# Modulation rows as column-tiled matmuls of four halves at once, made in the attentions and beside the context mixer

## The reference, cut to what matters

```
for l in range(2):                                       # first block
    mod = silu(c) @ w_ada[l] + b_ada[l]                  # 1024 x 6144
    sh_m, sc_m, gt_m, sh_f, sc_f, gt_f = split(mod, 6)
    h = rms_norm(x, g_pre_mix[l]) * (1 + sc_m) + sh_m
    x = x + gt_m * rms_norm(token_mixer(h), g_post_mix[l])
    h = rms_norm(x, g_pre_ffn[l]) * (1 + sc_f) + sh_f
    x = x + gt_f * rms_norm(conv_glu_ffn(h), g_post_ffn[l])
for i in range(2):                                       # second block
    mod_l = split(silu(c) @ w_mod[i] + b_mod[i], 6)      # the tokens' rows
    mod_c = split(silu(c_ctx) @ w_mod[i] + b_mod[i], 6)  # the context's rows
    ...
```

## Time and profile before

| | us |
|---|---|
| median of three runs | 3613.68 (3610.74 to 3615.86) |
| the profiled execution | 3609.14 |
| its span, first to last instruction | 3607.8 |
| TensorE busy | 2909.2 (81%) |
| VectorE busy | 2291.7 (64%) |
| ScalarE busy | 1138.5 (32%) |
| mean granted clock of TensorE | 0.912 |
| DMA | 1108.81 MB, mean 307 GB/s |

### The profile page before, as it was taken

One profiled execution on the slowest core, in us unless ns is written; L12 is line 12 of the kernel. 1 busy time (PEld: TensorE's weight loads), 2 busy tenths in 40 slices (PEclk: granted clock), 3 DMA queues, 4 the chain that ended last, 5 costly groups with the idle time before them and its releaser, 6 DMA issues.

```text
span 3607.8 us, 30555 instructions
## 1 busy us (share of the span) xinstructions
PE 2909.2 (81%) x9361; PEld 1544.3 (43%) x9361; DVE 2291.7 (64%) x4831; ACT 1138.5 (32%) x2909; POOL 970.6 (27%) x852
## 2 busy tenths in 40 slices
PE   7778877688989678987778787799789788877776
PEld 2344356266533347834437233343354463322222
DVE  1356548699867758865764999544423459975444
ACT  2012122323222343312542444333322224443333
POOL 1000000222322123323321444344300015443332
PEclk9989987699989779998879999999988899999999
DMA  7756733499979658997765999899952259999997
GB/s 269 274 177 224 240 120 126 182 399 344 368 294 399 248 207 346 417 402 269 300 221 199 388 421 421 353 420 421 421 203 76 67 221 421 421 421 422 421 422 328
DMA packets 214630, 1108.81 MB, mean 307 GB/s; under 512 B 25101, under 2 KB 25473, under 8 KB 116161
## 3 DMA queue, kind: packets, MB, share of 16 engines
q0 software_dynamic: 114864, 818.96, 56.2%
q1 hardware_dynamic: 98752, 287.17, 21.9%
q10 hardware_dynamic: 848, 0.72, 0.1%
HBM read 1105.58 MB, written 1.05 MB: 307 GB/s over the span
## 4 chain that ended last, share of the span: by engine, by line
PE 36%; DMA 29%; DVE 25%; ACT 5%; issue 3%; POOL 1%; SPq 1%; ACTq 0%; DVEq 0%; POOLq 0%
DMA AR<-in_uv,AR 23%; PE PS L820 10%; DVE AR L2270 7%; PE PS L2201 5%; PE PS L2114 3%; PE PS L1156 3%; DMA AR<-in_w_in 2%; PE PS L1628 2%; PE PS L2212 2%; DVE AR L371 1%; PE PS L802 1%; DVE AR L2265 1%; PE PS L2352 1%; PE PS L1143 1%; DMA AR<-in_w_down 1%
## 5 line engine op out<-in xcount | busy, mean ns | idle before, releaser
L2320 POOL DMA_INDIRECT AR<-in_uv,AR x768 | 892.8, 1162 | 1592.9 <-PE PS L2201 647.9
L2270 DVE CUSTOM_DVE_ANT_0 AR<-AR 128x1024 f32<-128x1024 f32 x768 | 937.3, 1222 | 505.0 <-DMA AR<-in_uv,AR 501.5
L2201 PE MATMUL PS<-AR 128*128 128x512 f32 x2048 | 973.6, 624 | 284.5 <-ACT AR L2257 278.4
L2201 PEld LDWEIGHTS PS<-AR 128*128 128x128 f32 x2048 | 388.0, 197 | 863.5 <-ACT AR L2257 446.0
L820 PE MATMUL PS<-AR 128*128 128x512 f32 (+3 forms) x1080 | 465.6, 583 | 32.0 <-DMA AR<-in_w_in 22.0
L2239 ACT ACTIVATE AR<-AR 128x2 f32<-128x2 f32 x384 | 78.1, 203 | 1147.1 <-DVE AR L2270 1143.7
L1143 PE MATMUL PS<-AR 128*128 128x256 f32 x1408 | 327.0, 391 | 14.3 <-DMA AR<-in_w_up_lin 9.6
L820 PEld LDWEIGHTS PS<-AR 128*128 128x128 f32 x1080 | 203.3, 203 | 275.8 <-issue 227.8
L1143 PEld LDWEIGHTS PS<-AR 128*128 128x128 f32 x1408 | 271.3, 195 | 81.9 <-issue 20.3
L2257 ACT ACTIVATE AR<-C,AR 128x128 f32<-128x128 f32 (+1 forms) x614 | 241.0, 392 | 20.1
L371 DVE SCALAR_TENSOR_TENSOR AR<-AR,CC 128x512 f32<-128x512 f32 x252 | 191.6, 760 | 83.1 <-DMA AR<-in_w_ada 39.3
(11 more groups left out here) (240 smaller groups left out, 2677.7 us busy)
## 6 DMA issues: line engine op xcount, KB each, us to landing
AR<-in_w_ada SPq DMA_DIRECT2D x160, 256.0 KB
AR<-in_w_in SPq DMA_DIRECT2D x56, 512.0 KB
AR<-in_w_mod SPq DMA_DIRECT2D x96, 256.0 KB, 4.4
AR<-in_peer_w_q SPq DMA_DIRECT2D x48, 512.0 KB
AR<-in_w_mod SPq DMA_DIRECT2D x45, 512.0 KB, 12.9
AR<-in_w_up_act SPq DMA_DIRECT2D x44, 512.0 KB
AR<-in_w_up_lin SPq DMA_DIRECT2D x44, 512.0 KB
AR<-in_w_down SPq DMA_DIRECT2D x44, 512.0 KB
```

The source lines that it names most:

```text
L2201: ins = pe.eng.matmul(acc[i][hh], e.dg(x), e.buf(x)[:, 1024 + 512 * hh:1536 + 512 * hh], start=(x == e.on[False][i][0]), stop=(x == e.on[F ...
L2270: v.eng.tensor_tensor_reduce(e.buf(x)[:, 0:1024], e.buf(x)[:, 0:1024], norm2(e).H[e.tiles[x // 128]], 1.0, 0.0, ALU.mult, ALU.add, DT[x // ...
L2320: g.eng.indirect_dma_start(e.buf(x), None, D["uv"][e.l], bass.IndirectOffsetOnAxis(ap=idx_at(x // 16, x % 16, 1), axis=0)).then_inc(*land. ...
```

## The change

`Mods` of the first block and `KeepMods` go. A new class `Quads` makes four halves at once: in each of the four column tiles of one bank stands another half, so a step of it is four pieces (256 KB each) and four matmuls with 32 equal columns as weights, eight steps make four halves; then four bias matmuls, one copy of the bank by ScalarE, and one transfer of four rows into `BR` (two transfers where two vectors are in the columns). There are eight such quads:

- `keeps`, three quads, in place of keep1 and keep2: from step 11 of the context's mixer on, one step to each of its steps, seven places for the pieces.
- `early`, three quads: rows 2, 4, 3, 5 of layer 0 and 1, 0 of layer 1, issued in the attention of layer 0 and in the context's queries, 16 places in `SL`, free once the context's second norm is transposed. The first gathers wait for its last sum.
- `later`, two quads: rows 2, 4, 3, 5 of layer 1, in the attention of layer 1, two steps to each of the first five attention steps (`QUICK`), eight places in `SCt`.

`KeptAda` (after `KeptMods`) spreads the rows from partitions 96 to 127 of `BR`: those of the layer itself in its eight `w_out` steps, two steps of the job to each, and rows 1, 0 of layer 1 in the up part of layer 0. GpSimd clears these partitions first.

```diff
+        class Quads:
+            def sp(self, sp):
+                n = len(self.own)
+                for q, (r0, halves) in enumerate(self.quads):
+                    for kc in range(8):
+                        for g, (l, r) in enumerate(halves):
+                            i = self.piece(q, kc, g)
+                            sp.wait_ge(("quad", self.key, i - n) if i >= n else self.guard)
+                            sp.eng.dma_start(self.own[i % n], self.w[l][r, kc // 2, :, 512 * (kc % 2):512 * (kc % 2) + 512]).then_inc(
+                                *land.landed(f"quad{i % n}", "raw", self.key, i))
+                        yield
+            def pe(self, pe):
+                    bk = bank(pe, SIDE, "quad", self.key, q)
+                    for kc in range(8):
+                        for g, (l, r) in enumerate(halves):
+                            pe.wait_ge(("raw", self.key, i))
+                            pe.eng.matmul(bk[32 * g:32 * g + 32, :], CP[:, 32 * kc:32 * kc + 32] if q in self.pairs else
+                                          CC[:, self.of + kc:self.of + kc + 1].to_broadcast([128, 32]), self.own[i % n],
+                                          start=(kc == 0), stop=False).then_inc(*pe.done("quad", self.key, i))
+                        if kc == 7:
+                            for g, (l, r) in enumerate(halves):
+                                ins = pe.eng.matmul(bk[32 * g:32 * g + 32, :], ident[0:48, rr:rr + 1].to_broadcast([48, 32]),
+                                                    BR[0:48, :], start=False, stop=True)
+            def keep(self, a, q):
+                a.eng.activation(ROWS_Q, psum("quad", self.key, q), ACT.Copy).then_inc(*a.done("ev", "quad", self.key, q))
+                a.eng.dma_start(BR[r0:r0 + 4, :], ROWS_Q[0:128:32, :]).then_inc(*land.landed("keptq", "kept", self.key, q))
...
+        class KeptAda(KeptMods):
+            def spread_out(self, pe, q):
+                pe.wait_ge(self.made)
+                pe.eng.matmul(bk, ident[96:128, r:r + 1].to_broadcast([32, 128]), BR[96:128, :], start=True, stop=True)
...
+        def attended(lane, l, steps):
+            for i, _ in enumerate(steps):
+                lane.fill(1 + (i < QUICK[l]), "q")
+                yield ATT[l]
...
         def first_pe(pe, l):
-            pe.run(mods_of["first", l])
-            for i, _ in enumerate(lin_pe(pe, ("win", l), D["w_in"][l], 8, (0, 3656), [0, 1], LAT.tile, prep=n1, ring=FIRST[l],
-                            whole=HEAD[l])):
-                if i >= 4 * len(HEAD[l]):
-                    pe.fill()
-                yield CH
-            pe.flush()
+            for _ in lin_pe(pe, ("win", l), D["w_in"][l], 8, (0, 3656), [0, 1], LAT.tile, prep=n1, ring=FIRST[l], whole=HEAD[l]):
+                yield CH
...
+            pe.flush("c")
+            pe.run(mods_of["quads", l], "q")
+            pe.fill(1, "q")
             yield 1.0
...
-            for _ in stages(8, s1, s2, s3):
-                yield ATT[l]
+            yield from attended(pe, l, stages(8, s1, s2, s3))
+            pe.flush("q")
+            pe.run(mods_of["first", l])
...
             for _ in lin_pe(pe, ("wout", l), D["w_out"][l], 8, (0, 1024), [0, 1], LAT.tile, seen=seen, ring=FIRST[l],
                             whole=TAIL[l]):
-                yield CH
+                pe.fill(2)
+                yield CH
+            pe.flush()
...
         def experts_pool(g, e):
-                    g.wait_ge(("idx", e.key, x // 16), ("sum", e.key, b) if b is not None else None)
+                    g.wait_ge(("idx", e.key, x // 16), ("sum", e.key, b) if b is not None else
+                              mods_of["quads", 0].summed() if e.halved else None)
...
         def context(lane, even, queries, experts):
-            lane.run(Ready(keep1, keep2), "keep")
             for i, share in enumerate(even(lane, "c")):
                 if i == AHEAD - 1:
                     lane.run(cmods, "c")
-                lane.fill(1 if i >= AHEAD else 0, "keep")
+                if i == AHEAD + 7:
+                    lane.flush("c")
+                    lane.run(keeps, "keep")
+                lane.fill(1, "keep")
                 yield PACE * share
             lane.flush("keep")
             lane.run(cgate, "c")
             for share in queries(lane, of_ctx):
+                lane.fill(1, "q")
                 yield PACE * share
```

More of the change, by code:

```diff
@@ L1205, in first_pool @@
             n1, n2 = norm_of["f", l, 1], norm_of["f", l, 2]
[L1206 to L1209 removed]
+            for _ in lin(g, 8, (0, 3656), [0, 1], nothing, prep=n1):
                 yield CH
[L1211 removed]
             yield 1.0
@@ L1324, in s2 @@
                                  ("mm", "av", l, u - 2) if u >= 2 else None).then_inc(*a.done("ev", "pt", l, u, kt))
-            for _ in stages(8, s1, s2, nothing):
-                yield ATT[l]
+            yield from attended(a, l, stages(8, s1, s2, nothing))
+            a.flush("q")
+            a.run(mods_of["first", l])
             for t in range(2):
@@ L1503, in s3 @@
                 v.events["ev", "av", l, u] = v.last
-            for _ in stages(8, s1, s2, s3):
-                yield ATT[l]
+            yield from attended(v, l, stages(8, s1, s2, s3))
+            v.flush("q")
+            v.run(mods_of["first", l])
             rs = []
```

181 lines of the change are left out of this document (105 added, 76 removed).

## The result

The changed kernel takes 3534.59 us (3531.89 to 3538.84, four runs) against 3614.05 of the kernel before beside it: a ratio of 0.9782, 95% interval 0.9765 to 0.9799. The gain is 79 us where 45 was forecast. They are cut at the same instructions in both kernels (the start on TensorE of the last `w_in` matmul, the flips, the output projection's transposes, the first up and down matmul, the next norm's transposes), so their bounds in time differ. A forecast in brackets is its range.

A forecast was written before the change was run, and what follows sets the result against it. Bounds were read by stretch: TensorE in the first, TensorE, VectorE and DMA in layer 0's up part, DMA and TensorE in layer 1's projection, none in the attentions. Terms sum to -45 us: 3569 us median, range 3525 to 3625.

The forecast's parts named there:

- (a): Up to layer 0's last w_in matmul: -22 us (-38 to +8), TensorE net -16, VectorE waits -6.
- (f): Layer 1's norm and w_in projection: -19 us (-27 to -8), fewer matmuls, TensorE 98.9 us at 0.91 busy.
- rival 1: Both attentions take the moved work in for free and gains cost nothing: 3528 to 3532 us; chance 0.18.
- rival 4: The first stretch gives nothing because the order of loads eats the gain: 3599 us; chance 0.12.
- (b): From layer 0's last w_in matmul to the flips: -27 us (-33 to -12), context norm and flips released earlier.
- (c): Attention of layer 0: +8 us (-8 to +30), half the added matmuls hidden (+14), higher clock -6.
- (d): Output projection of layer 0: +14 us (+8 to +26), 8 spreads 8.5 us, waits for gain rows 5.6.
- (h): Output projection of layer 1: +14 us (+8 to +26), 8 spreads 8.5 us, waits for gain rows 5.6.
- (e): FFN up part of layer 0: -32 us (-42 to -18), 186 us expected; one gain there separately +2.
- (g): Attention of layer 1: +17 us (+3 to +32), 9 of unhidden matmuls, five steps some 3 us late, 7 back.
- Rival 2: No attention gap takes the groups, all at the lower clock: 48 and 32 us there, total 3624; chance 0.12.
- Rival 3: Too few places for the pieces' landing, (g) 44 us over forecast, (a) loses 35: 3648 us; chance 0.07.

The follow-up runs named there:

- m_oldkeeps: The changed kernel with the kept rows made the old way (keep1 and keep2 on VectorE beside the context's mixer) in place of `keeps`: 3558.4 us, 0.9859.
- g_gains: The changed kernel with gain rows fetched earlier, rows 2 and 4 ahead of the attention, row 5 ahead of the output projection: 3548.5 us, 0.9830.
- j_late2: The changed kernel with row 5 of each layer spread in the FFN's up part instead of the output projection, still two steps per projection step: 3523.7 us, 0.9766.
- vdp_thin: The kernel before with VectorE's multiply-adds and the modulation loads in 16 of 512 columns and the partition-summing matmul left out, waits kept: 3525.2 us.

## Why the prediction was right, and where it was off

The sign and the range held, and so did every term but (a) and (f), which lie outside their bounds; the size was short by 34 us. The total, 3534.6, is next to that of rival 1, but not by its mechanism: the attentions were not free, they cost 34 us (forecast 25), more than anything rival 1 allows. It came out so near by errors that offset one another: (a), (f) and the up part gave 44 us more than forecast, attention 0 and output projection 1 took 24 more.

- **(a), -42.5 for -22.** This term failed, beyond its bound, and the step that failed is the -6 for waits. TensorE's busy time fell by 18 us and its idle time by 24 (from 77 to 53, counted from 0). The busy part is near the forecast -16, but by another sum: the pairs were 41.7 us, the quads 34.3 with their bias groups and late pieces, so only 7 net, and another 7 are the main matmuls, shorter at the higher clock, which the forecast left out. Of the idle part, TensorE's waits for main weights fell from 16.2 us to 5.5 (`in_even_w_in` 9.7 to 1.1, `in_w_in` 6.5 to 4.4); the longest of them stood ahead of 110 us, where the forecast's window begins. Its other waits, for one step of VectorE's in the mixer (L1842, now L1909) above all, fell from 13.9 us there to 5.9. The loads of the kept rows, feared as rival 4, cost nothing: m_oldkeeps has the same length.
- **(b), -24.3 for -27.** Right, and for the reasons given: ScalarE's last kept row stood before the norm (16 us by m_oldkeeps), and ada0b's tail before the flips (the other 8, by difference). The transposes come 10 us behind the last product, 12 were forecast.
- **(c), +22.9 for +8.** The term was in its band, its make-up was not. The matmuls were to cost 14; they cost 8. The gathers' gate, put at nothing, makes VectorE wait 6.5 us, and bank 7's copy makes TensorE wait 7.0, both in the changed kernel's waits of 427 to 614 us (below). The clock gave back less than the 6 us counted: 0.78 to 0.80.

```profile
PE PS L639 <- ACT MOD L655: 7.0, 2, 5.9
...
DVE AR L2337 <- DMA AR<-in_uv,AR: 6.5, 1, 6.5
```

- **(d), +13.1 for +14 and (h), +22.9 for +14.** The spreads are on the path as said: in (d) the projection's matmuls go from 33.2 us, first start to last end, to 41.4. In (h) TensorE also waits 4.6 us for results to be taken out of bank 7 (0.86 and 3.71, above), which the forecast hadn't counted. The second part of the term was the wrong wait: VectorE does wait for gain rows, 8.6 us in two waits where 5.6 a layer were forecast, but g_gains shows no cost in it. What costs in its place is the residual behind the last spreads, 7 us in (d) and 9 in (h) by j_late2, its spreads' own 2.2 us included.
- **(e) and (i), -37.0 for -30.** The comparison with layer 1's up part was good: 182 us of TensorE where 179 were worked out, waits of 9.6 us for `w_up_lin` gone. The idle share was taken as 3%; it is under 1%, and the clock rose from 0.95 to 1.00.
- **(f), -35.5 for -19.** Failed, outside its bound. The step took a fixed busy share of 0.91 for TensorE once its load was less; the earlier trace rows give 112 of 128, 0.87, so the share isn't that of before either. What it missed is what made up the idle time: TensorE waited 15.5 us for `w_in`, in six waits, and in its chain stood three transfers of 17 to 19 us; both are gone. Over the whole stretch TensorE's busy time fell from 139.6 to 120.9 us, 12.9 of it the pairs and 7 the main matmuls at the higher clock, and its idle time from 26 to 9. Thin pieces and thin multiply-adds give 12.7 of the 35.5, the sums 5.8.
- **(g), +11.2 for +17.** Inside its range, but not by its parts. The matmuls, put at 9, gave 0.2 back when they were cut; late loads, put at 15, gave 6.8; the 7 that were counted back weren't tested apart. With both cut, 5.4 of the 11.2 us stay open.
- Rival 2 came in a small part only: about a fifth of the groups in attention 0 and over a quarter in attention 1 are at the lower clock (1.93 us, 1.76 foreseen), and the attentions and outputs together cost 70 us (22.9 + 13.1 + 11.2 + 22.9) for a forecast of 53 and the 100 from which it decides. Rival 3 didn't come: TensorE's matmuls waited 2.1 us for `w_ada` in attention 1 and 6.6 us for pieces in all. The weight loads ahead of them stood 19.9 us for pieces in all, just below the 20 that the prediction names as a sign of being wrong. Rival 5 neither. The rule that a change of tiling mode drains TensorE (the Trainium skill, TensorEngine Tiling (Array Packing), Key Properties) was given at most 0.08 us a group. Lone groups between other matmuls now take 1.00 from start to next start, against 0.93 in a row, so 0.07 each, under 5 us for 64: as allowed for, and far from a whole matmul.

## What to carry to other kernels

A background job costs what its engines work, and in addition what stands behind its waits on every in-order queue: loads behind an issue that waits for a place (up to 8.4 us at once here), a residual behind a result that isn't urgent (7 and 9). When such a job leaves a stretch, count the idle time that the chain charges to it, and the clock, not its busy time alone; when it enters one, look for what its last steps stand in front of, and let rows that are needed late be made late.

## What was not expected of the hardware

A cut of TensorE's work can lower its clock and bring no time: with the quads' matmuls in 16 columns, TensorE's busy time in attention 1 fell by 8.5 us, the granted clock from 0.88 to 0.74, and the stretch went from 115.0 to 114.8; whether the clock or the late pieces held it there, the runs don't separate. The other way round, with ada0b and ada1b out of (a) and (f), TensorE waited less, its clock rose from 0.94 to 0.98 and from 0.92 to 0.96, and its own matmuls became 5 and 7% shorter. It isn't the jobs' work on VectorE and the DMA engines as such: with nearly all of that cut and the waits left, the clock in (a) stayed at 0.94 (vdp_thin). Four column tiles side by side take 1.06 us at full clock, no more than one spreading matmul of 32x512 (1.12).
